# Row sums ahead of long waits on VectorE, and more idle products before the first routing, in a fused two-block forward pass on one core

## What is computed

```python
def peer_ffn(x, w_query, sub_keys, u_tab, v_tab):        # per block of 128 tokens
        q = (xi @ w_query).reshape(B, T, PEER_HEADS, 2, PEER_HALF)
        s = jnp.einsum('bthcd,cnd->bthcn', q, sub_keys).astype(jnp.float32)
        s_top, i_top = lax.top_k(s, PEER_TOPK)
        ...
        best, pos = lax.top_k(cand.reshape(B, T, PEER_HEADS, PEER_TOPK * PEER_TOPK), PEER_TOPK)
        ...
        u = u_tab[idx]
        h = jax.nn.gelu(jnp.einsum('bthkd,btd->bthk', u, xi).astype(jnp.float32), approximate=False)
        w = (gate * h).astype(xi.dtype)
        return jnp.einsum('bthk,bthkd->btd', w, v_tab[idx])
```

## Time and profile before

| | |
|---|---|
| runs, median (lowest to highest) | 2450.24 us (2447.18 to 2451.2) |
| the profiled execution, its own time | 2448.43 us |
| its span | 2446.6 us |
| granted TensorE clock, mean | 0.92 |
| busy: PE, DVE, ACT, POOL | 1988.2, 1096.7, 440.0, 976.6 us |
| bytes moved by DMA | 906.97 MB, mean 371 GB/s |
| of it by the gathers (512 of u, 512 of v) | 536.94 MB |

### The profile page before, as it was taken

One profiled execution on the slowest core, in us unless ns is written; L12 is line 12 of the kernel. 1 busy time (PEld: TensorE's weight loads), 2 busy tenths in 40 slices (PEclk: granted clock), 3 DMA queues, 4 the chain that ended last, 5 costly groups with the idle time before them and its releaser, 6 DMA issues.

```text
span 2446.6 us, 22110 instructions
## 1 busy us (share of the span) xinstructions
PE 1988.2 (81%) x7910; PEld 1017.0 (42%) x7910; DVE 1096.7 (45%) x2663; ACT 440.0 (18%) x1123; POOL 976.6 (40%) x1059
## 2 busy tenths in 40 slices
PE   8827998779989778998887999999999866655555
PEld 5523553225445325445333664444595432222221
DVE  6569648963465964445985343444311220000001
ACT  2311511111311111311111111232102210000000
POOL 0036756674646776555777544555100000000000
PEclk9868999999999999999999999999999977888887
DMA  6268999999999999999999999999896579999996
GB/s 225 95 266 319 397 408 409 409 409 406 408 365 409 409 409 409 405 387 373 409 409 409 409 409 409 409 409 409 295 393 225 200 295 427 425 427 427 427 427 261
DMA packets 217921, 906.97 MB, mean 371 GB/s; under 512 B 27840, under 2 KB 28352, under 8 KB 206032
## 3 DMA queue, kind: packets, MB, share of 16 engines
q0 software_dynamic: 147456, 536.94, 55.7%
q1 hardware_dynamic: 67088, 358.77, 36.7%
q10 hardware_dynamic: 3264, 9.80, 1.0%
HBM read 904.37 MB, written 1.05 MB: 370 GB/s over the span
## 4 chain that ended last, share of the span: by engine, by line
PE 43%; DMA 27%; DVE 20%; issue 4%; POOL 4%; ACT 2%; SPq 1%; DVEq 0%; ACTq 0%
PE psum L2064 14%; DMA rows<-in_peer_v,idx 12%; PE psum L1863 10%; DVE rows L1064 7%; PE psum L1871 7%; DMA rows<-in_w_e_gate 5%; DMA rows<-in_w_e_down 4%; DMA rows<-in_w_e_up 3%; PE psum L2227 3%; POOL rows L707 2%; POOL rows L719 2%; PE psum L1832 2%; PE psum L2250 1%; DVE work L947 1%; DVE work L948 1%
## 5 line engine op out<-in xcount | busy, mean ns | idle before, releaser
L2064 PE MATMUL psum<-rows,diag 128*128 128x512 f32 x2024 | 977.8, 628 | 212.1 <-ACT diag L1570 136.6
L1064 DVE CUSTOM_DVE_ANT_0 rows<-rows,psum 128x1024 f32<-128x1024 f32 x512 | 613.3, 1219 | 329.2 <-DMA rows<-in_peer_u,idx 316.5
L2064 PEld LDWEIGHTS psum<-rows,diag 128*128 128x128 f32 x2024 | 382.7, 198 | 739.3 <-issue 557.8
L707 POOL DMA_INDIRECT rows<-in_peer_u,idx x512 | 487.1, 951 | 414.3 <-DVEq L744 146.3
L719 POOL DMA_INDIRECT rows<-in_peer_v,idx x512 | 485.8, 949 | 336.8 <-PE psum L2064 217.4
L1863 PE MATMUL psum<-rows,work 128*128 128x512 f32 x544 | 238.5, 593 | 2.1 <-ACT work L1389 2.1
L1871 PEld LDWEIGHTS psum<-work,rows 128*128 128x128 f32 x1920 | 219.3, 193 | 12.4 <-issue 9.8
L1871 PE MATMUL psum<-work,rows 128*128 128x128 f32 x1920 | 219.8, 276 | 2.3 <-DMA rows<-in_w_in 2.3
L1570 ACT ACTIVATE diag<-ident,wgt 128x128 f32<-128x128 f32 x506 | 167.7, 389 | 290.9 <-DVE wgt L1072 290.9
L1389 ACT ACTIVATE work<-psum 128x512 f32<-128x512 f32 (+5 forms) x190 | 95.1, 516 | 670.5 <-PE psum L1871 216.8
L1330 DVE TENSOR_TENSOR work<-kept,psum 128x512 f32<-128x512 f32 x8 | 8.2, 1029 | 426.6 <-PE psum L2227 426.6
(11 more groups left out here) (305 smaller groups left out, 1385.0 us busy)
## 6 DMA issues: line engine op xcount, KB each, us to landing
rows<-in_w_in SPq DMA_DIRECT2D x64, 1024.0 KB, 10.5
rows<-in_w_e_up SPq DMA_DIRECT2D x28, 2048.0 KB, 22.2
rows<-in_w_e_down SPq DMA_DIRECT2D x25, 2048.0 KB, 21.8
rows<-in_w_e_gate SPq DMA_DIRECT2D x24, 2048.0 KB, 24.4
rows<-in_gla_w_in SPq DMA_DIRECT2D x24, 1024.0 KB, 10.1
rows<-in_peer_w_query SPq DMA_DIRECT2D x16, 1024.0 KB, 9.3
rows<-in_peer_u,idx POOLq DMA_INDIRECT x512, 12.9
rows<-in_peer_v,idx POOLq DMA_INDIRECT x512, 13.5
```

The source lines that it names most:

```text
L707: pool.indirect_dma_start(out=u_rows[:, n % RU, :], out_offset=None, in_=a["peer_u"][g // 2], in_offset=bass.IndirectOffsetOnAxis(ap=idx[: ...
L1064: V_.tensor_tensor_reduce(out=u, in0=u, in1=tokens, scale=1.0, scalar=0.0, op0=ALU.mult, op1=ALU.add, accum_out=hid[:, r:r + 1]).then_inc( ...
L2064: last = mm(psum[:, 6 + c, :], diag[:, at % DIAGS, :], v_rows[:, n % RV, c * BANK:(c + 1) * BANK], start=r == 0, stop=summed(n + 1) == sum ...
```

## The change

A set `LONG_WAITS` names eight waits of four kinds: `out1` of the MLA stage that runs beside rows, `o1` and `out1` of both GLA stages, and `s1` of the routings 1 to 3. At these, `got` calls more rows before DVE waits, up to the last one that needs no gelu that ACT has not yet been handed: `gelu_reach(n)` is n rounded up to a multiple of 8, plus 2. The calls that are taken early are not made again later. The order of the other engines does not change, but for PE's idle products before the first routing: 11 instead of 6.

```diff
+LONG_WAITS = ({("mla", 1, "out1")} | {("gla", t, name) for t in range(NT) for name in ("o1", "out1")}
+              | {("route", v, "s1") for v in range(1, 4)})
+
+
+def gelu_reach(n):
+
+    return -(-n // BLK) * BLK + LAG - LEAD - BLK
...
                 rows_done.upto(last_got[0] - (0 if key + (name,) in PAIR_FIRST else 1))
+                if key + (name,) in LONG_WAITS:
+                    rows_done.until(gelu_reach(ROW_TARGET[last_got[0] - 2]))
                 dve.wait_ge(emptied, last_got[0])
...
                 if v == 0:
-                    idle(6)
+                    idle(11)
```

## The result

The changed kernel takes 2442.11 us (median of 6 runs, 2438.68 to 2444.95), the kernel before 2448.36 us (6 runs, 2445.91 to 2451.20). The ratio is 0.9972 with a 95% interval of 0.9962 to 0.9982: 6.9 us faster, between 4.4 and 9.3. The forecast, 2434, lies 14.4 us under this median of before (16.5 us was the sum), so more than half of the expected gain is missing. The profiled execution is the longest of its six, 2444.95 us with a span of 2443.1. So I also compare the traces by the start of the last row sum (row 511), which is where the paced part ends: 1719.7 us before, 1712.7 now, 7.0 us sooner, as the ratio says. The rest of the span, without a part of the change in it, took 730.4 us against 726.9.

What follows compares the result with a forecast made beforehand. DMA bytes at 408 to 409 GB/s set the pace, except in a start-paced stretch and five dips worth 15.3 us. Terms 2.9 + 4.8 + 6.7 + 2.1 = 16.5 us gave 2431.9 us, as a median 2434; range 2428 to 2449.

Steps and rivals of the forecast that it cites:

- Idle products, 2.9 us: PE before the first routing's queries: five more idle products keep the clock up, so the queries run 2.9 us shorter.
- `o1`, 4.8 us: Both GLA stages: DVE takes two row sums into its wait, so all behind comes 2.4 us sooner each, 4.8 us.
- `out1` of GLA, 6.7 us: Both GLA stages: nine sums go into the wait, POOL issues gathers earlier, filling dips of 3.3 and 3.4 us.
- `s1`, 2.1 us for the third routing, 0 for the others: Routing searches: five sums fewer fill the third's dip at 1152 us, 2.1 us; first and second routing give 0.
- The queue that I took for cover: First routing: searches 4.9 us late, covered by at least 6.7 us of queue ahead of a gather, so 0 lost.
- the two signs of being wrong: The rate at the GLA stages stays under 370 GB/s, or a new dip opens behind routing 1.
- DVE is held by its own sums: Rival: DVE waits for gathers at routing 1 and each `out1`; 13.8 us slower, chance 0.09, small form 0.04.
- Demand is moved, not added: Rival: gathers taken ahead displace weight pieces and new dips open later; half the dips go, median 2440.5 us, chance 0.18.
- The rate of the dips is all there is: Rival: no dip is filled and only the clock counts; median 2447.3 us, chance 0.07.
- the rule of the Trainium skill that the prediction quoted: HBM to SBUF transfers bind near 358 GB/s for a core, leaving dips of 322 to 351 GB/s nothing to fill.
- The clock falls all the same: Rival: at the first queries PE's clock still falls, the sums do as forecast; 13.6 us, median 2436.7, chance 0.05.

## Why the prediction was wrong

The forecast was 16.5 us, in four terms. The changed kernel gives 6.9. Point by point:

- **Idle products, 2.9 us: the clock was right, but in the changed kernel not all of it came through.** The clock holds at 1.00 across the gaps of 0.55 and 0.74 us, the queries take 7.41 us, the five more delay nothing, and the first gather is issued at 144.8 for 147.7 us. Alone they bring 3.4 us (1.2 to 5.6). On top of three sums at `out1` 1.4 to 2.2 us of it are left, and on top of nine 0.2 (medians) to 1.8 us (ratios), and nothing by row 511.
- **`o1`, 4.8 us: the chain moved as worked out, the price was too high.** The last product ahead of the norm's output (L1164) starts at 683.58 for 689.50, 5.9 us sooner, where the one at the stage's start (L1152) was 3.5 us sooner: the difference is the 2.4. PE's stall is 0.39 us. Alone (with the idle products) it brings 6.1 - 3.4 = 2.7 us; on top of three sums at `out1` it brings 0.5 by the medians (2438.18 and 2437.72), 0.8 by row 511 (1709.7 and 1708.9) and 1.7 by the ratios.
- **`out1` of GLA, 6.7 us: here the main step failed.** It was "PE idles there as it did, but POOL has by then issued gathers that it held back, and these fill the dip". The lateness was foreseen well (L1169 "near 715", it is 714.58; the norm near 721.7, the transposes at 721.03). What it was compared with was the wrong time. I took PE's 724.92 of before as what had to be met, so that 721 counted as a gain of 3.2 us. But the 5.08 us stall ahead of that was the very one that the sums remove, and without it the transposes can come at 711.73: 721.03 is 9 us late. And POOL had not issued enough: its next gather of v hangs on the rows that PE works through behind the transposes, 8.60 us later, 2.7 of them because PE's clock had fallen in its longer stall, for which the sum had no term. (`wgt` was ready 27 us sooner, at 693.43 for 720.64, not 20.) So nine sums cost 3.9 us against three, and likely 2 us against none. With three the term is near the forecast: 9.8 - 3.4 = 6.4 us alone, 8.0 by the medians.
- **`s1`, 2.1 us for the third routing, 0 for the others.** Where the dips behind `out1` are not filled the sums bring 2.3 us (all three `s1` and `out1` of MLA together; that it's the third, the window at 1140 us says). With them filled they bring nothing (2437.72 us without, 2438.16 with). In the first routing the searches start at 383.1 us, 3.8 us before my 386.9. The queue that I took for cover did not hold: 1.7 us of bytes were lost at 460 to 500 us, against my "the rate of 408". In time it cost nothing that can be measured, for another reason than mine: the stage behind gave it back.
- **The sum: the terms don't add.** Alone they are 3.4, 2.7, 6.4 and 2.3 us, 14.8 in all, close to the 16.5. Together, with three sums at `out1`, they are 10.8: some 4 us are counted twice. And 3.9 us are lost to the nine sums in place of three. 14.8 - 4.0 - 3.9 = 6.9. The single terms are differences of runs and no surer than 2 to 3 us: by the medians they are 2.4, 3.8, 8.0 and 2.6, 16.9 in all, and 6 us are counted twice.

Of the two signs of being wrong that the prediction gave itself, the second came (a new dip behind routing 1) and the first behind `out1` alone (354 GB/s at 716 to 728 us, 323 at 1108 to 1132).

The rivals. *DVE is held by its own sums* was the mechanism, at the place and with the gather (row 193) that it named, but as a partial loss inside a gain and not as a slower kernel; its threshold, a DVE that stands longer than 6.7 us of queue, was passed at the first `out1`, where DVE is 10 us late against the kernel with six sums (714.58 and 704.62). It and the forecast were not exclusive, and I had priced them as if they were. *Demand is moved, not added* (2440.5 us) was the nearest in time, and its idea, that gathers taken ahead are missing later, is what the windows at 680 and 1064 us show; its reason, that they displace weight pieces, the traces speak against: their queue had moved 45.12 MB by 700 us before and 46.11 in the changed kernel, 50.71 and 51.32 by 744, and 66.59 by 1056 in both. *The rate of the dips is all there is* fell: 1152 us went from 339 to 410 GB/s, and with three sums the place behind `out1` from 320 to 408 (716 to 732 us). By the rule of the Trainium skill that the prediction quoted, none of this would have been possible. Another page of the Trainium skill, "Perfetto Trace Analysis" ("Roofline"), limits that rule to two active cores and gives a lone core some 120% of it. With that the traces here agree, at 408 to 411 GB/s in these stretches. *The clock falls all the same* fell too, at 1.00.

What stays open: whether the 4 to 6 us that are counted twice can be had too, by row gathers that run further ahead of the GLA stages' own chain. No run tried it. How the sums ahead of `out1` of MLA and of the second `s1` do by themselves was not tried either.

## What to carry to other kernels

Filling an engine's wait with work that itself waits for a DMA paid here up to the point where the filler's last wait ends with the old one (six sums) and lost beyond it (nine). Count the fillers whose inputs have landed by then, and stop there. Price a delay against when the result could be used once the other stalls are gone, not against when it was used before. And where transfers are issued by a chain of engines, the dips of one queue are not separate prizes, as they were not here (14.8 us alone, 10.8 together): measure the second only with the first already filled.

## What the runs showed of the hardware

Two things I had not expected.

A gather's time from issue to landing grows with what has been issued ahead of it. Row 193's took 11.7 us when issued at 704.8 and 14.5 us when issued at 698.9, so issuing it 5.9 us earlier made it land only 3.1 us earlier (713.4 for 716.5). Over all fourteen traces: in the five that had 1.6 MB of gathers issued and not yet moved at that moment it took 8.9 to 11.0 us, in the nine that had 1.95 to 2.22 MB 11.7 to 15.2.

And the DMA engines held 408 or 409 GB/s in all fourteen traces through the long stretches of rows (760 to 1040 and 1180 to 1690 us), at a granted PE clock of 0.50 or 0.68 as of 1.00 (411 GB/s at 720 to 724 and 1072 to 1076 us above). Where the rate is lower, little is left in the queue. From 300 to 1690 us, in steps of 2 us, the mean rate of each trace is 408 or 409 GB/s where 2 MB or more of gathers are issued and not yet moved, 310 to 383 where it is 0.5 to 1 MB, and 234 to 321 below that.
